# Gate and up of the dense layer by seven half-size products for eight, and the down projection by column halves

## The chip, the cores and the metric

The program runs on one core of one Trainium2 chip. The metric is the device time of one execution in microseconds (us); lower is better. All tensors are float32, and the profile lists every float32 matrix multiplication as two TensorE instructions, called records here: two weight loads (PEld) and two MATMULs (PE).

## The reference, cut to what matters

A model of two blocks. The second block has two layers; the first of them ends in a dense SwiGLU layer, and only that is touched. It works on 528 tokens (16 meta tokens and 512), width 1024, inner width 2816:

```
def swiglu(t, wg, wu, wd):
    return (jax.nn.silu(t @ wg) * (t @ wu)) @ wd

h = layer_norm(ALPHA * h + mix, ln1_g[i], ln1_b[i])
f = swiglu(h, ffn_w_gate[j], ffn_w_up[j], ffn_w_down[j])      # layer 0
h = layer_norm(ALPHA * h + f, ln2_g[i], ln2_b[i])
```

## The kernel before, in words

The program is a chain of stages. Each stage is a block with one instruction list for each engine, ordered by semaphores alone, and all engines meet at the block's end. The dense layer is `dense_ffn` (L2848), between `mix_layer` of layer 0 (L2713) and `project_and_attend` of layer 1 (L2351). It has two blocks.

**Up block.** The tokens stand as columns in `core.feat` (128 partitions, DK = 8 slices of the width, NTOK = 528 columns). The 2816 inner channels are FC = 22 chunks of 128. A chunk's weights, gate and up together, are 1 MB; `core.lead` holds two chunks, each in a buffer of its own, and `load_dense` (L2842) loads the first two during `mix_layer`. A hardware loop of 11 turns takes two chunks a turn. TensorE computes, for each chunk, gate and up (`a`) for both halves of the tokens (HALF = 264 columns): 4 banks of PSUM of 8 accumulated matmuls each, so 32 matmuls or 64 records a chunk (L2893). Two sets of four banks alternate. ScalarE applies SiLU to the gate (L2903), VectorE multiplies it by up and writes `hm` (L2911). SP loads the chunk after next when TensorE has left a buffer (L2873), and behind the last of them the down weights `wd`, in two column halves of 5.6 MB (L2877).

**Down block.** `norm` (`TokenNorm`, L2162) is the layer norm of a token tile. TensorE first multiplies the 16 meta tokens for both column halves of `wd` (L2930), then four token tiles of 128 with both halves in turn (L2938; 22 matmuls or 44 records of 512 columns into one bank). After each second half it transposes the tile normalised before (`norm.turn`, L2227). VectorE adds the residual (L2965), takes statistics (L2180) and normalises (L2186 to L2209); ScalarE takes roots and moves the transposes back to `core.feat` (L2219, L2235). SP loads the norm's gains (L2176) and the next stage's first weights into `core.lead` (L2348) at the block's start.

Elsewhere in this kernel `chunk_half` of `project_and_attend` (L2465) does the like of the up block, written out without a loop: 8 matmuls (16 records) of 264 columns, each time with one wait on a semaphore ahead and one increment behind, two banks in turn, ScalarE reading each (L2565), VectorE at work on a convolution (L2663).

Of the kernel before, what the change touches and what calls it, by code (L numbers as in the profile page):

```python
# [8 lines left out]
ACT = mybir.ActivationFunctionType  # L9
ALU = mybir.AluOpType  # L10
AX = mybir.AxisListType

P = 128
# [51 lines left out]
class Core:  # L65
# [2096 lines left out]
class TokenNorm:  # L2162
# [19 lines left out]
    def center(self, dve, n, mean_square=None):  # L2182
        t, r = self.rows[n]
        h, mv, rt = self.core.hid[0:r, t, :], self.mv[0:r, n, :], self.rt[0:r, n, :]
        dve.wait_ge(self.measured, 2 * n + 2)
# [26 lines left out]
    def normalize(self, dve, n, mean_square=None):  # L2212
        self.center(dve, n, mean_square)
        self.finish(dve, n)

    def root(self, act, n):
# [613 lines left out]
def quarter(g, rows=META):  # L2830
    return slice(g * (P // 4), g * (P // 4) + rows)
# [16 lines left out]
def dense_ffn(core, A, w_in, weights):  # L2848

    with ExitStack() as ctx:  # L2850
        sb = lambda name, *shape: core.sb(ctx, name, [P, *shape])
        w = core.lead[:, :, :].rearrange("p (b a) x -> p b a x", b=2)
        wd = sb("wd", 2, FC, BANK)
        hm = sb("hm", FC, NTOK)
        norm = TokenNorm(core, ctx, A, 2, [(TILES, META)] + ROWS[:TILES], core.feat)
        sg = norm.gb[:, :, 0:NTOK]
        wd_in = [core.sem("wd_in") for _ in range(2)]
        made, silu, taken, down, out, summed, small_made, small_out = (
            core.sem(x) for x in "made silu taken down out summed small_made small_out".split())

        def halves(ap):
            return ap.rearrange("p (a n) -> p a n", a=2)

        with ExitStack() as up:
            pp = core.ps(up, "pp", [P, 2, 2, 2, BANK])
            with core.block() as block:

                @block.sync
                def _(sp):
                    with sp.Fori(1, FC // 2) as r:  # L2870
                        for b in range(2):
                            sp.wait_ge(made, r * 2 + b + 1)
                            sp.dma_start(w[:, b, :, :].rearrange("p a x -> p (a x)"),  # L2873
                                         A["ffn_up_2"][bass.ds(r * 2 + b, 1)].rearrange("c p x -> p (c x)")).then_inc(w_in[b], 16)
                    wdv = A["ffn_down_2"].rearrange("(f p) n -> p f n", p=P)
                    for half in range(2):
                        sp.dma_start(wd[:, half, :, :], wdv[:, :, half * BANK:(half + 1) * BANK]).then_inc(wd_in[half], 16)  # L2877

                @block.gpsimd
                def _(pool):  # L2880
                    core.clear_retired(pool)

                @block.tensor
                def _(pe):
                    pe.sem_inc(made, 2)
                    with pe.Fori(0, FC // 2) as r:
                        for b in range(2):
                            pe.wait_ge(w_in[b], r * 16 + 16)
                            pe.wait_ge(taken, r * 2 + b + 1)
                            for a in range(2):  # L2890
                                for half in range(2):
                                    for k in range(DK):
                                        last = pe.matmul(pp[:, b, a, half, 0:HALF], w[:, b, a, k * P:(k + 1) * P],  # L2893
                                                         core.feat[:, k, half * HALF:(half + 1) * HALF], start=k == 0, stop=k == DK - 1)
                            last.then_inc(made, 1)

                @block.scalar
                def _(act):
                    with act.Fori(0, FC // 2) as r:
                        for b in range(2):  # L2900
                            act.wait_ge(made, r * 2 + b + 3)
                            act.wait_ge(taken, r * 2 + b + 1)
                            act.activation(halves(sg[:, b, :]), pp[:, b, 0, :, 0:HALF], ACT.Silu).then_inc(silu, 1)  # L2903

                @block.vector
                def _(dve):
                    dve.sem_inc(taken, 2)  # L2907
                    with dve.Fori(0, FC // 2) as r:
                        for b in range(2):
                            dve.wait_ge(silu, r * 2 + b + 1)  # L2910
                            dve.tensor_tensor(halves(hm[:, bass.ds(r * 2 + b, 1), :].rearrange("p a n -> p (a n)")),  # L2911
                                              halves(sg[:, b, :]), pp[:, b, 1, :, 0:HALF], ALU.mult).then_inc(taken, 1)

        po = core.ps(ctx, "po", [P, TILES, BANK])
        pm = core.ps(ctx, "pm", [P, 2, BANK])
        turned = core.ps(ctx, "turned", [P, 2, BANK])
        banks = [turned[:, a, :] for a in range(2)]
        with core.block() as block:

            @block.sync  # L2920
            def _(sp):
                norm.load(sp)
                weights.load(sp)

            @block.tensor
            def _(pe):
                for half in range(2):
                    pe.wait_ge(wd_in[half], 16)
                    for f in range(FC):
                        last = pe.matmul(pm[quarter(f % 4), half, :], hm[:, f, row_cols(TILES)], wd[:, half, f, :],  # L2930
                                         start=f < 4, stop=f >= FC - 4)
                    last.then_inc(small_made, 1)
                for n in range(2 * TILES):
                    t, half = divmod(n, 2)
                    if n >= TILES:
                        pe.wait_ge(out, n - TILES + 1)
                    for f in range(FC):
                        last = pe.matmul(po[:, n % TILES, :], hm[:, f, row_cols(t)], wd[:, half, f, :],  # L2938
                                         start=f == 0, stop=f == FC - 1)
                    last.then_inc(down, 1)  # L2940
                    if half:
                        norm.turn(pe, t, banks)
                norm.turn(pe, TILES, banks)

            @block.scalar
# [7 lines left out]
            @block.vector  # L2953
            def _(dve):
                for half in range(2):
                    dve.wait_ge(small_made, half + 1)
                    add_quarters(dve, core.hid[0:META, TILES, half * BANK:(half + 1) * BANK], pm[:, half, :], summed, half, small_out)
                    dve.wait_ge(small_out, half + 1)
                    norm.take_stats(dve, 0, half)
                norm.normalize(dve, 0)  # L2960
                for n in range(2 * TILES):
                    t, half = divmod(n, 2)
                    dve.wait_ge(down, n + 1)
                    h = core.hid[:, t, half * BANK:(half + 1) * BANK]
                    dve.scalar_tensor_tensor(out=h, in0=h, scalar=ALPHA, in1=po[:, n % TILES, :],  # L2965
                                             op0=ALU.mult, op1=ALU.add).then_inc(out, 1)
                    dve.wait_ge(out, n + 1)
                    norm.take_stats(dve, t + 1, half)
                    if half:
                        norm.normalize(dve, t + 1)  # L2970


UT = P // 2
# [635 lines left out]
```

## Time and profile before

| | us |
|---|---|
| runs | 3224.13, 3210.89, 3216.73 |
| median of the 3 runs | 3216.73 |
| span of the profiled execution, first to last instruction | 3206.7 |
| its own time | not given; the span is 10.0 below the median |
| up block's matmuls, L2893 | 1611.9 to about 1927.8 |
| down block, L2930 to the last transpose | 1929.7 to about 2102 |

A row of the profile names line, engine, operation, the tile written and the tiles read, then count, busy time and mean duration. Durations of matmuls overlap each other (a MATMUL of 386 ns starts every 0.22 us), so the pace is read from starts, not from durations. PEclk is the granted TensorE clock as a share of full speed (1.00 is 2.4 GHz, 0.50 is 1.2 GHz, between them a mix of the two).

### The profile page before, as it was taken

The page shows a single profiled execution, that of the slowest core. Times are in us where ns is not written, and L with a number is a line of the kernel's source. Part 1 is how long each engine was busy: PE and PEld are TensorE (multiplying, and loading weights), DVE is VectorE, ACT ScalarE, POOL GpSimd, SP SyncE. Part 2 cuts the span into 40 slices and gives each one's busy share as a digit, 9 for nine tenths or more (in the row PEclk, how much of TensorE's full clock was granted, in tenths as well). Part 3 has the DMA queues.
Part 4 walks back from the last instruction along what each step waited for, and adds up shares of the span by engine and source line. Part 5 has one row for each costly group of instructions (what it writes and reads, how often), then busy time and mean ns, then how long its engine had stood idle before and what let it go on. Part 6 is the DMA issues. An engine that isn't in the chain of part 4 may idle for free. (4 is left out here: it accounts for less than half of the span.)

```text
span 3206.7 us, 43786 instructions
## 1 busy us (share of the span) xinstructions
PE 2981.5 (93%) x18418; PEld 1840.9 (57%) x18418; DVE 1047.9 (33%) x1946; ACT 549.4 (17%) x1262; POOL 220.6 (7%) x204
## 2 busy tenths in 40 slices
PE   8998899998779979989999999999999799999897
PEld 5544788654343338867578884478776444444343
DVE  5666665653311233731400002109222311111014
ACT  3222333221111121133000000011240000000001
POOL 0001321340000000011000000000010100000000
PEclk9998899999879979999999999999999799999998
DMA  3411000116289931202012142011220614547917
GB/s 115 107 53 44 4 17 26 43 40 248 120 338 431 426 111 47 105 27 118 0 53 78 66 162 86 0 55 72 78 94 1 271 50 203 232 171 320 414 49 290
DMA packets 79478, 414.04 MB, mean 129 GB/s; under 512 B 10675, under 2 KB 16179, under 8 KB 63588
## 3 DMA queue, kind: packets, MB, share of 16 engines
q1 hardware_dynamic: 68028, 384.75, 30.3%
q10 hardware_dynamic: 7848, 14.61, 1.9%
q0 software_dynamic: 3456, 12.58, 1.0%
q8 instruction: 110, 1.80, 0.2%
q14 instruction: 36, 0.29, 0.0%
HBM read 383.17 MB, written 28.76 MB: 128 GB/s over the span
## 5 line engine op out<-in xcount | busy, mean ns | idle before, releaser
L3318 PE MATMUL pgu<-gu,xg 128*64 128x320 f32 (+1 forms) x2560 | 393.4, 462 | 8.9 <-POOLq L3246 8.9
L2893 PE MATMUL pp<-feat,lead 128*128 128x264 f32 x1408 | 315.8, 388 | 2.0 <-DVEq L2907 2.0
L3318 PEld LDWEIGHTS pgu<-gu,xg 128*64 128x64 f32 x2560 | 182.3, 137 | 204.7 <-issue 130.3
L2893 PEld LDWEIGHTS pp<-feat,lead 128*128 128x128 f32 x1408 | 269.0, 191 | 48.7 <-DVEq L2907 2.3
L312 PE MATMUL proj<-feat,w 128*128 128x512 f32 x576 | 254.4, 595 | 2.6 <-PEq L153 2.6
L2465 PE MATMUL ring<-feat,lead 128*128 128x264 f32 x1024 | 243.3, 397 | 3.0 <-PEq L2253 1.5
L2465 PEld LDWEIGHTS ring<-feat,lead 128*128 128x128 f32 x1024 | 198.1, 196 | 40.4 <-issue 6.2
L3325 PE MATMUL py<-down,hm_t 128*64 128x512 f32 x880 | 200.3, 603 | 10.0 <-POOLq L3246 10.0
L2465 PE MATMUL ring<-feat,w 128*128 128x264 f32 x896 | 209.4, 390 | 0.0
L2465 PEld LDWEIGHTS ring<-feat,w 128*128 128x128 f32 x896 | 169.1, 192 | 30.3 <-issue 2.4
L312 PEld LDWEIGHTS proj<-feat,w 128*128 128x128 f32 x576 | 106.7, 190 | 123.8 <-issue 123.8
L497 DVE SCALAR_TENSOR_TENSOR mixed<-padded,taps,mixed 128x512 f32<-128x512 f32 x216 | 162.4, 752 | 7.7
L2663 DVE SCALAR_TENSOR_TENSOR conv<-vg,cols,conv x240 | 163.3, 760 | 0.0
L2938 PE MATMUL po<-wd,hm 128*128 128x512 f32 x352 | 151.9, 593 | 0.0
L3325 PEld LDWEIGHTS py<-down,hm_t 128*64 128x64 f32 x880 | 62.0, 139 | 121.4 <-issue 104.6
L3387 DVE TENSOR_TENSOR hm<-sg,pgu 128x384 f32<-128x384 f32 (+1 forms) x40 | 20.8, 521 | 314.7 <-PE pgu L3318 209.1
L2911 DVE TENSOR_TENSOR hm<-gb,pp 128x528 f32 x22 | 15.5, 704 | 305.1 <-ACT gb L2903 305.1
L2938 PEld LDWEIGHTS po<-wd,hm 128*128 128x128 f32 x352 | 66.6, 190 | 83.2 <-issue 83.1
L2778 PE MATMUL pp<-wo,feat 128*128 128x512 f32 x256 | 111.3, 593 | 2.8 <-POOL feat L2827 2.8
L3270 ACT ACT_TABLE_LOAD x19 | 24.4, 1283 | 460.8 <-PE pgu L3318 280.3
L2778 PEld LDWEIGHTS pp<-wo,feat 128*128 128x128 f32 x256 | 48.1, 190 | 61.9 <-issue 61.9
L2219 ACT ACTIVATE rt<-rt 128x1 f32<-128x1 f32 (+1 forms) x15 | 3.0, 203 | 378.1 <-DVE rt L2189 378.1
(493 smaller groups left out, 3479.2 us busy)
## 6 DMA issues: line engine op xcount, KB each, us to landing
gu<-in_moe_gu SPq DMA_DIRECT2D x16, 3072.0 KB, 13.4
gu<-in_moe_gu SPq DMA_DIRECT2D x16, 2560.0 KB, 15.8
ring<-in_w_gate SPq DMA_DIRECT2D x16, 2048.0 KB, 13.6
ring<-in_w_up SPq DMA_DIRECT2D x16, 2048.0 KB, 15.5
ring<-in_w_down SPq DMA_DIRECT2D x16, 2048.0 KB, 17.7
w<-in_w_in SPq DMA_DIRECT2D x15, 2048.0 KB, 7.7
down<-in_moe_down SPq DMA_DIRECT2D x8, 3072.0 KB
lead<-in_ffn_up SPq DMA_DIRECT2D x22, 1024.0 KB, 4.8
```

What stands on the lines that cost most here:

```text
L312: last = pe.matmul(proj[:, n % 2, :], w[:, g % 2, k, c * P:(c + 1) * P], core.feat[:, k, :], start=k == 0, stop=k == DK - 1)
L497: dve.scalar_tensor_tensor(out=out, in0=src[:, j:j + SEQ], scalar=taps[:, n, j:j + 1], in1=out, op0=ALU.mult, op1=ALU.add).then_inc(convol ...
L2465: last = pe.matmul(ring[:, n % RINGS, 0:HALF], w[g % 2][:, c, k * P:(k + 1) * P], core.feat[:, k, cols(half)], start=k == 0, stop=k == DK - 1)
L2663: dve.scalar_tensor_tensor(out=out, in0=src[:, j:j + NTOK], scalar=tap(c, j), in1=out, op0=ALU.mult, op1=ALU.add).then_inc(own, 1)
L2778: last = pe.matmul(pp[:, n % 2, n // 2 % 2, 0, :], mixed[:, k, row_cols(t)], wo[:, k, half * BANK:(half + 1) * BANK], start=k == 0, stop=k ...
L2893: last = pe.matmul(pp[:, b, a, half, 0:HALF], w[:, b, a, k * P:(k + 1) * P], core.feat[:, k, half * HALF:(half + 1) * HALF], start=k == 0, ...
L2911: dve.tensor_tensor(halves(hm[:, bass.ds(r * 2 + b, 1), :].rearrange("p a n -> p (a n)")), halves(sg[:, b, :]), pp[:, b, 1, :, 0:HALF], AL ...
L2938: last = pe.matmul(po[:, n % TILES, :], hm[:, f, row_cols(t)], wd[:, half, f, :], start=f == 0, stop=f == FC - 1)
L3270: act.activation(sg[:, q, 0:n], pgu[:, 2 * q, 0:n], ACT.Silu).then_inc(silu, 1)
L3318: last = pe.matmul(pgu[half(h), part, 0:n], xg[:, k, :], w[:, k, h, :], start=k == 0, stop=k == DK - 1)
L3325: last = pe.matmul(py[half(h), :], hm_t[:, c, :], down[:, c, h * BANK:(h + 1) * BANK], start=c == 0, stop=c == XC - 1)
L3387: dve.tensor_tensor(hm[:, c0:c0 + n], sg[:, q, 0:n], pgu[:, 2 * q + 1, 0:n], ALU.mult).then_inc(multiplied, 1)
```

## The change

Two chunks of channels and two halves of the width and of the tokens make 2 x 2 x 2 blocks. In place of eight half-size products, seven are computed for gate and seven for up for each pair of chunks, on sums and differences of the weight blocks and of the token blocks (Strassen's method, in Winograd's form). Each product is 4 matmuls (8 records) of 264 columns. Three of the bank groups are read by ScalarE in the middle of the accumulation (a copy into SBUF), and more products are then added to the same bank; VectorE adds the copies to later contents.

For each pair: TensorE 14 products; ScalarE 6 copies and 4 SiLUs; VectorE 6 sums of a copy and a bank, 3 multiplications, and 4 sums of weight blocks (1024 elements a partition each). Once at the start VectorE forms 4 sums of token blocks (1056 elements each). The 11 pairs are written out, with no hardware loop. A second weight buffer `w_second` is added, and a pair is one load of 2 MB. The first half of the down weights (`wd0`) is loaded at the up block's start; the second (`wd1`) at the down block's start, ahead of the gains and the next stage's weights. The down block does all first column halves (meta, then four tiles), then all second halves. `core.feat`'s block x12 is overwritten by a difference; the temporaries lie in the norm's gain buffer.

The diff, cut to its core:

```diff
 def load_dense(core, A, sp, landed):
     for b in range(2):
...
-                     A["ffn_up_2"][b:b + 1].rearrange("c p x -> p (c x)")).then_inc(landed[b], 16)
+                     A["ffn_up_2"][b:b + 1].rearrange("c p x -> p (c x)")).then_inc(landed[0], 16)
...
                 def _(sp):
-                    with sp.Fori(1, FC // 2) as r:
-                        for b in range(2):
-                            sp.wait_ge(made, r * 2 + b + 1)
-                            sp.dma_start(w[:, b, :, :].rearrange("p a x -> p (a x)"),
...
-                    for half in range(2):
-                        sp.dma_start(wd[:, half, :, :], wdv[:, :, half * BANK:(half + 1) * BANK]).then_inc(wd_in[half], 16)
+                    load_pair(1)
+                    sp.dma_start(wd0[:, :, :], wdv[:, :, 0:BANK]).then_inc(wd_in[0], 16)
+                    for r in range(2, PAIRS2):
+                        sp.wait_ge(product, PRODUCTS * (r - 1))
+                        load_pair(r)
...
                 def _(pe):
-                    with pe.Fori(0, FC // 2) as r:
-                        for b in range(2):
-                            pe.wait_ge(w_in[b], r * 16 + 16)
-                            pe.wait_ge(taken, r * 2 + b + 1)
-                            for a in range(2):
-                                for half in range(2):
-                                    for k in range(DK):
...
+                    def multiply(bank, lhs, rhs, a, begin):
+                        for k in range(KH):
+                            last = pe.matmul(bank, lhs[:, a, k * P:(k + 1) * P], rhs[:, k, :], start=begin and k == 0,
+                                             stop=k == KH - 1, skip_group_check=True)
+                        last.then_inc(product, 1)
+
+                    for r in range(PAIRS2):
+                        pe.wait_ge(w_in[r % 2], 16 * (r // 2 + 1) + (16 if r % 2 == 0 else 0))
+                        if r >= 2:
+                            pe.wait_ge(opened, OPENED * (r - 2) + O21 + 1)
+                            pe.wait_ge(hidden, HIDDEN * (r - 2) + H21 + 1)
+                        for a in (GATE, UP):
+                            multiply(bank_x(r, a), weight(r, 0, 0), x11, a, True)
+                        if r:
+                            pe.wait_ge(added, SUMS * (r - 1) + S11_U + 1)
+                        for a in (GATE, UP):
+                            multiply(bank_y(a), weight(r, 0, 1), x21, a, True)
+                        pe.wait_ge(w_summed, 4 * r + 2)
+                        pe.wait_ge(x_summed, 2)
+                        for a, c in ((GATE, C1_G), (UP, C1_U)):
+                            pe.wait_ge(copied, COPIES * r + c + 1)
+                            multiply(bank_x(r, a), s2(r), t2, a, False)
+                        for a, c in ((GATE, S12_G), (UP, S12_U)):
+                            if r:
+                                pe.wait_ge(added, SUMS * (r - 1) + c + 1)
+                            multiply(bank_z(a), s1(r), t1, a, True)
+                        pe.wait_ge(w_summed, 4 * r + 4)
+                        pe.wait_ge(x_summed, 3)
+                        for a, c in ((GATE, C2_G), (UP, C2_U)):
+                            pe.wait_ge(copied, COPIES * r + c + 1)
+                            multiply(bank_x(r, a), s3(r), t3, a, False)
+                        for a, c in ((GATE, C5_G), (UP, C5_U)):
+                            pe.wait_ge(copied, COPIES * r + c + 1)
+                            multiply(bank_z(a), s4(r), x22, a, False)
+                        pe.wait_ge(x_summed, 4)
+                        for a, c in ((GATE, S22_G), (UP, S22_U)):
+                            pe.wait_ge(added, SUMS * r + c + 1)
+                            multiply(bank_x(r, a), weight(r, 1, 1), t4, a, False)
...
                 def _(act):
...
+                        copy(r, G_P1, c1[GATE], bank_x(r, GATE))
+                        copy(r, U_P1, c1[UP], bank_x(r, UP))
+                        act.wait_ge(added, SUMS * r + S11_G + 1)
+                        act.activation(c1[GATE], c1[GATE], ACT.Silu).then_inc(opened, 1)
+                        copy(r, G_P6, c2[GATE], bank_x(r, GATE))
+                        copy(r, U_P6, c2[UP], bank_x(r, UP))
+                        copy(r, G_P5, c5[GATE], bank_z(GATE))
+                        copy(r, U_P5, c5[UP], bank_z(UP))
...
                 def _(dve):
...
+                    sum_weights(0, (0, 1))
+                    sum_inputs()
+                    sum_weights(0, (2, 3))
+                    for r in range(PAIRS2):
+                        add(r, G_P2, C1_G, c1[GATE], bank_y(GATE))
+                        add(r, U_P2, C1_U, c1[UP], bank_y(UP))
+                        add(r, G_P7, C5_G, c5[GATE], bank_x(r, GATE))
+                        add(r, U_P7, C5_U, c5[UP], bank_x(r, UP))
+                        add(r, G_P3, C2_G, c2[GATE], bank_z(GATE))
+                        add(r, U_P3, C2_U, c2[UP], bank_z(UP))
+                        open_and(r, O22, S22_U)
+                        dve.tensor_tensor(hm[:, 2 * r + 1, HALF:], c5[GATE], c5[UP], ALU.mult).then_inc(hidden, 1)
+                        open_and(r, O12, S12_U)
+                        dve.tensor_tensor(hm[:, 2 * r, :], row1[GATE], row1[UP], ALU.mult).then_inc(hidden, 1)
+                        if r + 1 < PAIRS2:
+                            sum_weights(r + 1, (0, 1))
+                        dve.wait_ge(opened, OPENED * r + O21 + 1)
+                        dve.wait_ge(product, PRODUCTS * r + U_P4 + 1)
+                        dve.tensor_tensor(hm[:, 2 * r + 1, 0:HALF], open21, bank_x(r, UP), ALU.mult).then_inc(hidden, 1)
+                        if r + 1 < PAIRS2:
+                            sum_weights(r + 1, (2, 3))
...
             def _(sp):
+                sp.dma_start(wd1[:, :, :], wdv[:, :, BANK:]).then_inc(wd_in[1], 16)
                 norm.load(sp)
                 weights.load(sp)
...
-                for n in range(2 * TILES):
-                    t, half = divmod(n, 2)
-                    if n >= TILES:
-                        pe.wait_ge(out, n - TILES + 1)
...
+                    for t in range(TILES):
+                        if half:
+                            pe.wait_ge(out, t + 1)
+                        for f in range(FC):
+                            last = pe.matmul(po[:, t, :], hm[:, f, row_cols(t)], wd[half][:, f, :], start=f == 0, stop=f == FC - 1)
```

`bank_x(r, a)` is bank 2a + r % 2, `bank_y(a)` bank 4 + a, `bank_z(a)` bank 6 + a. `sum_weights(r, ...)` first waits for the pair's load and for the last product of the pair before that reads its targets (`U_P3`), then forms s1, s2, s4 and s3 in that order.

## Rows read from the trace of the kernel before

**Rows 1.** The page's part 1: busy us, share of the span, instructions.
```profile
PE 2981.5 (93%) x18418; PEld 1840.9 (57%) x18418; DVE 1047.9 (33%) x1946; ACT 549.4 (17%) x1262; POOL 220.6 (7%) x204
```
**Rows 2.** Windows, all engines: stretch, us, busy (x count) each, PEclk, DMA share, GB/s.
```profile
1612.00:1928.00 316.00, 315.76 (x1408) 268.95 (x1408) 14.79 (x21) 27.07 (x33) 0.00 (x0) 0.99 0.27 96
1928.00:1941.00 13.00, 10.45 (x88) 2.70 (x88) 4.11 (x6) 1.77 (x2) 0.00 (x0) 1.00 1.03 399
1941.00:2100.00 159.00, 155.34 (x390) 70.33 (x389) 28.99 (x46) 4.16 (x13) 0.00 (x0) 1.00 0.00 1
```
**Rows 3.** Timeline of ScalarE in the up block: start, us, line, operation, idle before.
```profile
1628.84 1.28 ACT L2903 ACT_TABLE_LOAD   x1 [17.80 <-PE pp L2893]
...
1913.62 1.28 ACT L2903 ACT_TABLE_LOAD   x1 [13.61 <-PE pp L2893]
...
1927.88 0.61 ACT L2903 ACTIVATE gb<-pp 128x528 f32<-128x528 f32 x1 [12.35 <-PE pp L2893]
```
**Rows 4.** Windows of L2893 alone: stretch, us, PE busy, PEld busy, PEclk, DMA.
```profile
1612.00:1640.50 28.50, 28.50 (x118) 24.00 (x119) 0.92 0.11 38
...
1657.30:1685.78 28.48, 28.48 (x130) 24.32 (x129) 1.00 0.21 74
```
**Rows 5.** Timeline of layer 0's projection: products of 16 records, written out, with VectorE busy.
```profile
1319.71 15.07 PE L2465 MATMUL ring<-feat,lead 128*128 128x264 f32 x67
1319.87 19.77 DVE L2663 SCALAR_TENSOR_TENSOR conv<-vg,cols,conv  x29
...
1320.58 0.39 ACT L2565 ACTIVATE gates<-ring 128x264 f32<-128x264 f32 x1 [3.17 <-PE ring L2465]
...
1341.94 0.39 ACT L2565 ACTIVATE gates<-ring 128x264 f32<-128x264 f32 x1 [3.17 <-PE ring L2465]
```
**Rows 6.** Windows of L2465 alone, the same stretch: columns as in rows 4.
```profile
1310.00:1345.00 35.00, 35.00 (x159) 29.90 (x158) 1.00 0.36 127
```
**Rows 7.** Groups by line and shape, whole span: VectorE and ScalarE operations of like size.
```profile
L1880 DVE TENSOR_TENSOR feat<-slot_t,hid 128x1024 f32<-128x1024 f32 x4 | 4.6, 1220 | 0.0
L2648 DVE TENSOR_TENSOR vg<-vg 128x528 f32<-128x528 f32 x8 | 5.7, 709 | 123.2 <-ACT vg L2565 123.2
L2671 DVE SCALAR_TENSOR_TENSOR conv<-ring,conv 128x264 f32<-128x264 f32 x16 | 5.8, 425 | 37.4 <-PE ring L2481 37.4
L1568 DVE TENSOR_TENSOR steps_and_weighted<-cst,scal 128x512 f32<-128x512 f32 x32 | 34.0, 1105 | 0.0
L2565 ACT ACTIVATE gates<-ring 128x264 f32<-128x264 f32 x64 | 24.8, 388 | 137.5 <-PE ring L2465 137.5
```
**Rows 8.** The page's part 6, loads: out<-in, queue, count, size, median us to landing.
```profile
w<-in_w_in SPq DMA_DIRECT2D x15, 2048.0 KB, 7.7
...
wd<-in_ffn_down SPq DMA_DIRECT2D x2, 5632.0 KB, 27.5
```
**Rows 9.** One line's own view, L2877 (the down weights' two loads): shortest, median, longest.
```profile
L2877 SPq DMA_DIRECT2D wd<-in_ffn_down x2: 390/5211/10032, 1900.0 to 1900.4; - x2
...
DMA to landing us min/median/max: 19.7/27.5/35.4
```
**Rows 10.** Timeline where the up block ends and the down block begins.
```profile
1928.63 0.70 DVE L2911 TENSOR_TENSOR hm<-gb,pp 128x528 f32 x1 [12.26 <-ACT gb L2903]
...
1929.72 5.33 PE L2930 MATMUL pm<-wd,hm 128*16 128x512 f32 x44 [1.96 <-PEq L2866]
...
1935.88 5.33 PE L2930 MATMUL pm<-wd,hm 128*16 128x512 f32 x44 [0.83 <-DMA wd<-in_ffn_down]
...
1941.14 38.03 PE L2938 MATMUL po<-wd,hm 128*128 128x512 f32 x88
```
**Rows 11.** Waits from 1600 to 2110: who for whom, us in total, times, longest.
```profile
DVE hid L2965 <- PE po L2938: 128.3, 8, 17.5
```
**Rows 12.** Windows, all engines, around the start of layer 1's projection: columns as in rows 2.
```profile
2100.00:2110.00 10.00, 8.52 (x28) 6.72 (x27) 0.00 (x0) 1.48 (x3) 0.20 (x1) 0.66 0.57 211
2110.00:2150.00 40.00, 40.00 (x181) 34.15 (x181) 1.42 (x2) 5.59 (x12) 0.00 (x0) 1.00 0.15 53
```

More of the change, by code:

```diff
@@ L2855, in dense_ffn @@
         norm = TokenNorm(core, ctx, A, 2, [(TILES, META)] + ROWS[:TILES], core.feat)
-        sg = norm.gb[:, :, 0:NTOK]
+        kept = norm.gb[:, :, :].rearrange("p a d -> p (a d)")
         wd_in = [core.sem("wd_in") for _ in range(2)]
[L2858 to L2862, printed above, removed]
-        with ExitStack() as up:
-            pp = core.ps(up, "pp", [P, 2, 2, 2, BANK])
+        down, out, summed, small_made, small_out = (core.sem(x) for x in "down out summed small_made small_out".split())
@@ L2897, in _, with copy @@
                 @block.scalar
                 def _(act):
[L2899 to L2903, printed above, removed]
+                    def copy(r, j, dst, bank):
+                        act.wait_ge(product, PRODUCTS * r + j + 1)
+                        act.activation(dst, bank, ACT.Copy).then_inc(copied, 1)
@@ L2905, in _, with sum_weights @@
                 @block.vector
                 def _(dve):
[L2907 to L2912, printed above, removed]
+                    def sum_weights(r, steps):
+                        for n in steps:
+                            if n == 0:
+                                dve.wait_ge(w_in[r % 2], 16 * (r // 2 + 1) + (16 if r % 2 == 0 else 0))
+                                if r:
+                                    dve.wait_ge(product, PRODUCTS * (r - 1) + U_P3 + 1)
+                                dve.tensor_tensor(s1(r), weight(r, 1, 0), weight(r, 1, 1), ALU.add).then_inc(w_summed, 1)
+                            else:
+                                dve.wait_ge(w_summed, 4 * r + n)
+                                out, x, y = {1: (s2(r), s1(r), weight(r, 0, 0)), 2: (s4(r), weight(r, 0, 1), s2(r)),
+                                             3: (s3(r), weight(r, 0, 0), weight(r, 1, 0))}[n]
+                                dve.tensor_tensor(out, x, y, ALU.subtract).then_inc(w_summed, 1)
@@ new lines, in sum_inputs, with add @@
+                    def sum_inputs():
+                        for n, (out, x, y) in enumerate(((t1, x12, x11), (t2, x22, t1), (t3, x22, x12), (t4, x21, t2))):
+                            if n:
+                                dve.wait_ge(x_summed, n)
+                            dve.tensor_tensor(out, x, y, ALU.subtract).then_inc(x_summed, 1)
+                    def add(r, j, c, dst, bank):
+                        dve.wait_ge(product, PRODUCTS * r + j + 1)
+                        dve.wait_ge(copied, COPIES * r + c + 1)
+                        dve.tensor_tensor(dst, dst, bank, ALU.add).then_inc(added, 1)
@@ L2914, in dense_ffn @@
+        wd1 = sb("wd1", FC, BANK)
+        wd = (wd0, wd1)
         po = core.ps(ctx, "po", [P, TILES, BANK])
@@ L2929, in _ @@
                     for f in range(FC):
[L2930 removed]
+                        last = pe.matmul(pm[quarter(f % 4), half, :], hm[:, f, row_cols(TILES)], wd[half][:, f, :],
                                          start=f < 4, stop=f >= FC - 4)
                     last.then_inc(small_made, 1)
[L2933 to L2942 removed]
+                    for t in range(TILES):
[3 more added lines that the diff above has]
+                            last = pe.matmul(po[:, t, :], hm[:, f, row_cols(t)], wd[half][:, f, :], start=f == 0, stop=f == FC - 1)
+                        last.then_inc(down, 1)
+                        if half:
+                            norm.turn(pe, t, banks)
                 norm.turn(pe, TILES, banks)
@@ L2959, in _ @@
                     norm.take_stats(dve, 0, half)
[L2960 to L2968, printed above, removed]
-                    if half:
-                        norm.normalize(dve, t + 1)
+                    if half:
+                        norm.normalize(dve, 0, taken=len(norm.rows) + 1)
+                    for t in range(TILES):
+                        n = half * TILES + t
+                        dve.wait_ge(down, n + 1)
+                        h = core.hid[:, t, half * BANK:(half + 1) * BANK]
+                        dve.scalar_tensor_tensor(out=h, in0=h, scalar=ALPHA, in1=po[:, t, :],
+                                                 op0=ALU.mult, op1=ALU.add).then_inc(out, 1)
+                        dve.wait_ge(out, n + 1)
+                        norm.take_stats(dve, t + 1, half)
+                        if half:
+                            norm.normalize(dve, t + 1, taken=len(norm.rows) + t + 2)
 UT = P // 2
```

82 lines of the change are left out of this document (70 added, 12 removed).

## Prediction

> **What bounds the kernel now.** I read the page's busy shares first: TensorE is busy 93% of the span, VectorE 33%, ScalarE 17% [rows 1]. A mean says nothing of one stage, so the windows come next. In the up block TensorE is busy 315.76 of 316 us, VectorE 14.8, ScalarE 27.1, DMA 0.27 of its time; the down block is the same picture [rows 2]. So a record taken from TensorE is time taken from the end, as long as the rest, which grows a lot, stays hidden.
>
> Then the pace. The table loads of SiLU come once a loop turn; eleven of them lie between 1628.84 and 1913.62, so a turn is 284.78 / 10 = 28.48 us [rows 3]. It holds 128 records (two chunks of 64): 0.2225 us a record, at a clock of 1.00 [rows 4]. The first 28.5 us hold 118 records where a later turn's window counts 130, at 0.92 [rows 4]: a start at the lower level that costs 12 x 0.2225 = 2.7 us, before and after alike.
>
> **What is removed.** The new pair has 14 products of 4 matmuls, 14 x 8 = 112 records for 128; 11 pairs have 1232 for 1408. The shape stays 128x264, so 176 x 0.2225 = 39.2 us go.
>
> **Many small groups.** The new code waits and increments about every 8 records (154 times; before, 22 times). No row has groups of 8 records of this shape. Nearest is the projection: written out, a wait and an increment every 16 records, two banks read by ScalarE in turn, VectorE at work on SBUF beside it. ScalarE's reads are (1341.94 - 1320.58) / 6 = 3.56 us apart, again 0.2225 a record, at 1.00 [rows 5, 6]. So waits long satisfied cost nothing I can see at 16, and neither does loop against written-out code. Lower bound 0: the loop shows no overhead to win back. Upper bound: one handover a product. From ScalarE's SiLU (ends 1928.49) to VectorE's start at 1928.63 that is 0.14 us [rows 3, 10]; 154 x 0.14 = 21.6 us. I take 0, since the projection is by far the likest row.
>
> The Trainium skill, TensorE: Matmul & The Clock Gate, section The cost: per-tile semaphore tail, says that increments of matmuls finish one after another, 26.3 ns each. By that, 132 more increments would cost an estimated 3.5 us and the gain would be 3.5 us smaller; the trace does not bear it out for matmuls that follow one another, since one increment in 16 records and one in 64 run at the same pace [rows 3, 5].
>
> **What is added beside TensorE.** The pair takes 112 x 0.2225 = 24.9 us, a product 1.78. I count from the pair's start; product n ends at 1.78n, in the order P1, P2, P6, P5, P7, P3, P4, each gate then up.
>
> ScalarE: 6 copies and 4 SiLUs of 264 elements at 0.39 [rows 7], 3.9 us of 24.9. VectorE: 6 sums and 2 multiplications of 264 at 0.43, one of 528 at 0.71, 4 weight sums of 1024 at 1.22 [rows 7]: 3.4 + 0.7 + 4.9 = 9.0 us. Neither is near 24.9, so only the order can hurt:
> - P6 gate (starts 7.1) adds to the bank of P1 gate. The copy is done by 1.8 + 0.4 + two handovers = 2.5. Slack 4.6.
> - P7 gate (14.2) needs the copy of P6 gate (ends 8.9): about 9.6. Slack 4.6. P3 gate (17.8) needs the copy of P5 gate (12.5): 13.2.
> - P4 gate (21.4) needs VectorE's sum of P7 gate (16.0): 16.7. Slack 4.7.
> - The next pair's P6 (at 24.9 + 7.1 = 32.0) needs s1 and s2, which VectorE may begin once P3 up has ended (21.4). In front of them stand a sum, a multiplication of 264 and one of 528; with the two sums 0.43 + 0.43 + 0.71 + 2.44 = 4.0 of 10.6 us. s3 and s4 follow P4 up: 24.9 + 0.43 + 2.44 = 27.8, wanted at 39.1.
> - First pair: s1, s2 and four token sums (1056 elements; I take 1.25) and s4, s3 are 9.9 us before VectorE takes its first add. P6 wants the first four by 7.1 (4.9), P7 all by 14.2. Behind them ScalarE's SiLU and the copy of P6 gate come at 9.9 + 0.43 + 0.39 + 0.39 = 11.1, some 11.6 with handovers. Slack 2.6, the tightest place, and the low clock there adds to it. Here lies the far bound of a VectorE sum: the slowest SBUF sum in the trace is 1.105 us for 512 elements [rows 7], so 2.2 for 1024. Eight of them end at 17.7, and P7 would be some 5 us late, once; in later pairs 6.0 of 10.6 still fits.
>
> So everything added is priced at nothing, covered by TensorE's 24.9 us a pair; if the cover went, its price would be each lateness itself, pair by pair.
>
> **Loads.** A pair is 2 MB. Such loads land in 7.7 us [rows 8], and pair r+1's buffer is asked for at the start of pair r and wanted at 21.4: slack 13.7. At the block's start SP issues pair 1 and then wd0, 5.6 MB; one of the two down loads, issued together, landed in 19.7 us, though SP was held 10.0 us in issuing one of them [rows 9]. The queue is free before pair 2 is asked for at 24.9. In the down block wd1 is issued at its start, ahead of the gains and the next stage's weights; it has the meta rows, 5.3 us, and four tiles at 38.03 / 2 = 19.0 each [rows 10], 81 us, and wants about 20. The gains behind it are needed after that too. The next stage wants its weights some 165 us on.
>
> **The seams.** Before, the last product was followed by SiLU (1927.88) and a multiplication ending 1929.33 [rows 3, 10], 1.5 us after the last product. Now the gate's SiLU runs beside P4 up, and one multiplication of 264 remains: 0.43 plus a handover. 1.0 us goes. TensorE's wait of 0.83 us for the second down half goes as well [rows 10]. A second change from meta rows to full tiles is added; the row shows 1935.88 + 5.33 to 1941.14, no gap, so 0 [rows 10]. In the down block VectorE waited 128.3 us for TensorE [rows 11], TensorE never for VectorE; with the halves apart, a bank is read four tiles before it is reused, and the last tile's normalisation has the same length. 0. The start of the up block has fewer registers to set and a longer code; TensorE's idle at the like seam is 1.96 us [rows 10], so between 2 us won and 2 lost; I take 0.
>
> **Sum.** 39.2 + 1.0 + 0.8 = 41.0 us. The profiled span, 3206.7, becomes 3165.7. That execution's own time is not given; its span lies 10.0 below the median of the runs, 3216.73, and I carry that over: 3175.7 us. About 0.5% (16 us) is what a measurement of this kernel tells from no change.
>
> **Rivals.**
> 1. *Each group pays a handover.* TensorE does not run ahead over the waits, and each product begins 0.14 us late: 21.6 us back, 3197.3. For it: no row has groups as short. Against: the projection [rows 5, 6]. Chance 0.10.
> 2. *The chain through VectorE and ScalarE becomes the bound* (slower than before). Place: each pair's s1 and s2 for the next P6, or in the first pair the sums before P7. It decides once TensorE loses over 41.0 / 11 = 3.7 us a pair, so when the 4.0 us of VectorE's work in that place take 14.3, 3.6 times my rows. At four times, 16.0 us, 5.4 are lost a pair, 59 in all: 3235. Against: the worst row gives 6.0. Chance 0.03.
> 3. *The clock falls.* At the lower level a record takes twice as long, so 184 of the 1232 records at that level eat the whole gain. The level was mixed, 0.66, where TensorE started after a break, and 1.00 in the next stretch [rows 12]; if each pair had idling enough to run 30 of its records so, 11 x 30 x 0.2225 = 73 us are lost, 3249. Against: rows 5 and 6 change banks each 3.56 us at 1.00. Chance 0.03. The Trainium skill, TensorE: Matmul & The Clock Gate, section A second HAM failure mode: psum-queue depth-cycling, has this rule: going round PSUM's banks with small idle times between groups makes the clock swing and takes throughput. By that rule this rival would be the outcome; rows 5 and 6 disagree so far.
> 4. *A load comes late, or the gain is lost elsewhere.* 2 MB would have to take 21.4 us for a first stall; within 0.5%: 3217. Chance 0.02.
> 5. *The change does not do what it says:* counted in the code, 14 calls of 4 matmuls a pair leave 112 records; chance under 0.01, in rival 4.
>
> The forecast keeps 0.82.
>
> **How the numbers follow.** Forecast 3175.7. Low end: the start's 2.0, and the 5.8 by which the lowest run lies below the median: 3168. High end: the handover's whole bound, 3197. Forecast and rival 1 make 0.92 faster, and of the rest a mild form of 2 or 3 leaves some gain: faster 0.93, same 0.03, slower 0.04.
>
> **What would show it.** L2893's successor with 1232 records, and the first SiLU's of two pairs 24.9 us apart; a clock of 1.00 from the second pair on; TensorE's idle inside the block near 0, with at most a piece in the first pair; the block's matmuls ending near 1888.6; no wait for `wd`. A spacing of 26.9 would be rival 1; idle time on TensorE put down to `sums_w` or `kept` rival 2; PEclk under 0.95 rival 3; idle put down to a DMA rival 4.

## The result and the profile after

The changed kernel takes 3177.33 us (median of 4 runs, 3173.29 to 3178.81), the kernel before 3214.92 beside it (4 runs). The ratio is 0.9879, 95% interval 0.9864 to 0.9893. Forecast was 3175.7, in a range of 3168 to 3197. The profiled execution took 3173.29 us around a span of 3171.5.

The windows of the changed kernel's dense layer, all engines (columns as in [rows 2]): the up block, the first meta rows, the rest of the down block.

```profile
1618.00:1895.00 277.00, 276.83 (x1232) 235.77 (x1232) 99.11 (x146) 45.35 (x111) 0.00 (x0) 0.99 0.26 97
1895.00:1901.00 6.00, 5.08 (x45) 1.43 (x44) 0.43 (x1) 1.28 (x1) 0.00 (x0) 1.00 0.65 208
1901.00:2068.00 167.00, 162.43 (x438) 72.64 (x436) 32.41 (x51) 5.04 (x15) 0.00 (x0) 0.99 0.12 46
```

Against [rows 2]: 1408 records in 316 us have become 1232 in 277. TensorE is as full as it was. VectorE has gone from 14.8 us to 99.1 in that stretch and ScalarE from 27.1 to 45.4, and neither is seen in TensorE's time. That is the whole change in one row.

The timeline around the first change of pairs, weight loads left out (start, us, engine, line, operation, idle before):

```profile
1618.17 1.23 DVE L3019 TENSOR_TENSOR sums_w<-lead 128x1024 f32<-128x1024 f32 x1 [2.66 <-PEq L2741]
1618.17 9.90 PE L2947 MATMUL pp<-feat,lead 128*128 128x264 f32 x32 [1.49 <-PEq L2741]
...
1624.96 1.28 ACT L2996 ACT_TABLE_LOAD   x1
...
1626.87 1.22 DVE L3024 TENSOR_TENSOR lead<-lead 128x1024 f32<-128x1024 f32 x1
...
1629.89 0.39 ACT L2988 ACTIVATE gb<-pp 128x264 f32<-128x264 f32 x1 [1.00 <-PE pp L2947]
...
1635.03 3.72 PE L2947 MATMUL pp<-feat,lead 128*128 128x264 f32 x16
...
1643.66 1.22 DVE L3019 TENSOR_TENSOR sums_w<-w_second 128x1024 f32<-128x1024 f32 x1
...
1644.92 1.22 DVE L3024 TENSOR_TENSOR sums_w<-sums_w,w_second 128x1024 f32<-128x1024 f32 x1
1645.71 7.28 PE L2947 MATMUL pp<-feat,w_second 128*128 128x264 f32 x32
...
1647.76 0.39 ACT L2988 ACTIVATE gb<-pp 128x264 f32<-128x264 f32 x1 [3.23 <-PE pp L2947]
...
1652.83 7.28 PE L2947 MATMUL pp<-sums_x,sums_w 128*128 128x264 f32 x32
...
1654.81 0.39 ACT L2988 ACTIVATE gb<-pp 128x264 f32<-128x264 f32 x1 [2.67 <-PE pp L2947]
...
1659.95 3.72 PE L2947 MATMUL pp<-feat,w_second 128*128 128x264 f32 x16
...
1872.03 0.39 ACT L2988 ACTIVATE gb<-pp 128x264 f32<-128x264 f32 x1 [3.23 <-PE pp L2947]
```

Read it as a set of deadlines. The second pair's P1 begins at 1645.71; VectorE ends s2 at 1644.92 + 1.22 = 1646.14, 0.43 us after that, and P6, which needs it, begins at 1652.83: 6.7 us to spare. The room is smaller for the copy of P6 gate: it ends at 1654.81 + 0.39 = 1655.20, and P7, which needs it, begins at 1659.95, 4.75 us later. In the first pair the eight sums end at 1628.09, 9.9 us after the block's start, and P6 gate's copy ends at 1630.28, 4.75 us before P7 at 1635.03. The copies of P1 gate in pairs two and eleven, 1647.76 and 1872.03, are nine pairs apart: 24.92 us a pair, 0.2225 a record. The one idle time in the list of TensorE is that of the block's start. The granted clock is 0.88 from 1618 to 1640, where the first 32 records take 9.90 us and later ones 7.28, and 1.00 from 1640 to 1895.

The seams, where the up block ends and where the layer ends:

```profile
1895.18 0.43 DVE L3059 TENSOR_TENSOR hm<-gb,pp 128x264 f32<-128x264 f32 x1 [2.24 <-PE pp L2947]
...
1896.00 5.33 PE L3082 MATMUL pm<-wd,hm 128*16 128x512 f32 x44 [0.92 <-PEq L2925]
...
1901.26 49.19 PE L3089 MATMUL po<-wd,hm 128*128 128x512 f32 x114
...
2065.12 1.97 PE L2227 MATMUL turned<-cst,hid 128*128 128x128 f32 x8 [3.65 <-DVE hid L2209]
...
2068.57 6.65 PE L2465 MATMUL ring<-feat,lead 128*128 128x264 f32 x17 [1.48 <-PEq L3069]
```

TensorE's idle at the seam is 0.92 where it was 1.96 [rows 10], and the wait for `wd` is gone.

Stage by stage, from these starts (before: 1611.9, 1929.7, 2102.1, span 3206.7):

| stretch | before | after | difference |
|---|---|---|---|
| start to the up block's first matmul | 1611.9 | 1618.2 | +6.2 |
| up block to down block | 317.8 | 277.8 | -40.0 |
| down block to layer 1's projection | 172.4 | 172.6 | +0.2 |
| from there to the end | 1104.6 | 1102.9 | -1.7 |
| span | 3206.7 | 3171.5 | -35.2 |

The layer itself gives 39.8 us. The 6.2 us ahead of it, in code that is the same in both, want an explanation, and so does the 0.2 in the down block. The last row needs none: over thirteen profiles of all kernels here that stretch takes between 1102.7 and 1106.7 us, in either kernel.

### The profile page after: what moved, and what is told of

It is laid out like the page before. It is cut to its first block and busy times, and to the rows that moved or that the text cites. A ratio compares the mean times of both kernels' runs of the same rounds, so it can differ in the third digit from the quotient of the medians.

```text
span 3171.5 us, 43527 instructions
## 1 busy us (share of the span) xinstructions
PE 2946.1 (93%) x18242; PEld 1809.0 (57%) x18242; DVE 1131.1 (36%) x2071; ACT 567.5 (18%) x1340; POOL 221.1 (7%) x204
## 5 line engine op out<-in xcount | busy, mean ns | idle before, releaser
L2465 PE MATMUL ring<-feat,lead 128*128 128x264 f32 x1024 | 242.6, 397 | 3.0 <-PEq L3069 1.5
L2465 PEld LDWEIGHTS ring<-feat,lead 128*128 128x128 f32 x1024 | 197.6, 196 | 40.4 <-issue 6.3
L2465 PE MATMUL ring<-feat,w 128*128 128x264 f32 x896 | 209.4, 390 | 0.0
L2465 PEld LDWEIGHTS ring<-feat,w 128*128 128x128 f32 x896 | 169.1, 192 | 30.3 <-issue 2.4
L3035 DVE TENSOR_TENSOR gb<-gb,pp 128x264 f32<-128x264 f32 x66 | 28.2, 429 | 174.8 <-PE pp L2947 174.8
L2947 PE MATMUL pp<-sums_x,sums_w 128*128 128x264 f32 x352 | 80.1, 386 | 0.0
L2947 PEld LDWEIGHTS pp<-sums_x,sums_w 128*128 128x128 f32 x352 | 66.9, 190 | 11.4
```

What stands on the lines that cost most here:

```text
L2465: last = pe.matmul(ring[:, n % RINGS, 0:HALF], w[g % 2][:, c, k * P:(k + 1) * P], core.feat[:, k, cols(half)], start=k == 0, stop=k == DK - 1)
L2947: last = pe.matmul(bank, lhs[:, a, k * P:(k + 1) * P], rhs[:, k, :], start=begin and k == 0, stop=k == KH - 1, skip_group_check=True)
L3035: dve.tensor_tensor(dst, dst, bank, ALU.add).then_inc(added, 1)
```

## The experiments

My theory: TensorE's count of records is the time, and all that was added is covered with slack that can be counted. The rivals: the gain comes in part from elsewhere (the loop's removal, the order of the down block); or the cover is thin (groups, sums, reads or loads near their limit); or stops bring the clock down.

**The kernel before once more (e1_before_again).** No edit.

> The kernel before, unchanged, for a second profile. The changed kernel's profile reached the dense layer 6.2 us later than the first profile of before did, in code that is the same in both. If that is scatter of the earlier stages, this profile begins the up block's matmuls somewhere from 1611 to 1619 us; if the new program costs time ahead of the layer (longer code, other loads), it begins within 1 us of 1611.9. Up block start to down block start 317.8 us, down block start to the projection of layer 1 172.4 us, both within 0.5 us: these hold no scatter by either theory.

Measured: one run of 3218.81 us, span 3217.1. The view of L2893 alone:

```profile
L2893 PE MATMUL pp<-feat,lead x1408: 385/386/803, 1621.8 to 1937.4; 128*128 128x264 f32 x176
```

The unchanged kernel reaches the layer at 1621.8, 9.9 us later than in its first profile and 2.8 beyond the range that I had given scatter. Over thirteen profiles of all kernels here that start lies between 1611.9 and 1624.9, for forms of the kernel before between 1611.9 and 1621.8, for forms of the changed one between 1612.9 and 1624.9. So the 6.2 us lie within the scatter of the stages before, and the first profile of before reached the layer earliest of all. A cost of the new program of a microsecond or two ahead of the layer could not be told from that scatter. The up block again takes 317.9 us. The down block took 173.4, a microsecond over what I expected, for the reason at the end of this section.

**The down block's order alone (e2_down_order_alone)**, in the kernel before:

```diff
-                for n in range(2 * TILES):
-                    t, half = divmod(n, 2)
+                    for t in range(TILES):
```

> The kernel before with only the down block's order changed (all first column halves, then all second; loads as before). My theory: only TensorE's wait of 0.83 us for the second half of wd goes, so down block start to layer 1's projection falls from 172.4 us to 171.6, and the time stays within 0.1% of before. A rival, that the order itself is worth some of the gain (less waiting on normalisation), would show 5 us or more below before.

Measured: 3213.58 us, ratio 1.0005 (0.9995 to 1.0015). The wait for `wd` is gone, yet the down block takes 172.6 us (1930.8 to 2103.4) and not the 171.6 expected; 0.88 of that microsecond is the last transposes, told of below. The order by itself is worth nothing that the runs could show.

**The old order in the changed kernel (e3_old_down_order)**: the same lines turned back, `wd1` still loaded at the block's start.

> The changed kernel with the old order of the down block (tile by tile, both halves), the second half of wd still loaded at the down block's start. My theory: TensorE needs wd1 5.3 us after the block's start and it lands after about 15 to 20 us (19.7 us with another load of its size beside it before), so TensorE stands idle 10 to 14 us once, and after that break the clock is low for some us more: 12 to 17 us slower than the changed kernel, 3190 us. The rival, that the order does not matter since loads are fast enough, expects under 3 us.

Measured: 3186.61 us, ratio 0.9928 (0.9911 to 0.9944), about 0.5% or 16 us above the changed kernel's ratio. The timeline of that down block:

```profile
1890.71 5.33 PE L3082 MATMUL pm<-wd,hm 128*16 128x512 f32 x44 [0.92 <-PEq L2925]
...
1908.69 6.75 PE L3082 MATMUL pm<-wd,hm 128*16 128x512 f32 x44 [12.65 <-DMA wd<-in_ffn_down]
```

TensorE stands 12.65 us, and the 44 records behind the stop take 6.75 us where they took 5.33. The down block is 185.6 us, 13 to 14 more than in the changed kernel. So the new order has a job: not to save time, but to let `wd1` be loaded so late. In the code the second weight buffer and the sums are given back at the up block's end, and `wd1` is laid out only then.

**The loop written out, nothing else (e4_before_written_out):**

```diff
-                    with pe.Fori(0, FC // 2) as r:
+                    for r in range(FC // 2):
```

and so on SP, ScalarE and VectorE.

> The kernel before with the up block's hardware loop written out on all four engines, nothing else. My theory: the loop costs nothing, 128 records in 28.48 us with or without it; up block start to down block start 317.8 us give or take 0.5, time as before within 0.2%. The rival, that part of the 40 us gained in the up block is the loop's branches and the table load it repeats, expects 5 us or more less.

Measured: 3215.03 us, ratio 1.0008 (0.9999 to 1.0018); the up block 317.7 us. One table load is left of eleven, and the up block is no shorter for it. None of the gain is the loop's.

**Four more sums a pair (e5_four_more_sums)** in the place where P6 waits for VectorE:

```diff
+                                for n in range(4 if r else 0):
+                                    dve.tensor_tensor(s1(r), weight(r, 1, 0), weight(r, 1, 1), ALU.add).then_inc(again, 1)
+                                    dve.wait_ge(again, 4 * (r - 1) + n + 1)
```

> The changed kernel with VectorE forming s1 five times instead of once in each pair after the first: 4 more sums of 1024 elements, 1.26 us each, in the place where the next pair's P6 waits. My theory, from the changed kernel's profile: s2 ends 0.43 us after the pair's first record and P6 begins at 7.12; with 4 x 1.26 = 5.0 more it ends at 5.5, still in time, so nothing changes: 112 records in 24.92 us, time as the changed kernel's, ratio to before 0.988. The rival, that VectorE's added work already costs TensorE something (reads of SBUF beside it, or waits close to their limit), expects the pair to lengthen by 0.3 us or more, 3 us in all.

Measured: 3171.84 us, ratio 0.9869 (0.9853 to 0.9886), the up block 277.9 us. Doubling VectorE's sums of weights costs nothing.

**Eight more (e6_eight_more_sums):** the same with 8.

> The same with 8 more sums, 10.1 us: s2 ends at 10.5, P6 wanted it at 7.12. My theory of the chain: TensorE stands idle 3.4 to 3.6 us in each of 10 pairs, 35 us in all, and no other wait appears (VectorE's sum of P2 comes at 13.9, the copy of P6 gate at 14.7, P7 gate at 17.8). With the rival of the clock on top, each such stop lets the granted clock fall to the lower level for some us after it, and a pair loses 5 to 7 us, 50 to 70 in all, with PEclk under 0.9. If neither, the idle time is under 2 us a pair.

Measured: 3220.1 us, ratio 1.0021 (1.0009 to 1.0032): the whole gain is gone, and a little more. The up block takes 325.1 us (1617.41 to 1942.5), 47.3 more. TensorE's timeline at three of the ten P6:

```profile
1655.52 9.07 PE L2948 MATMUL pp<-sums_x,sums_w 128*128 128x264 f32 x32 [3.28 <-DVE sums_w L3028]
1685.67 7.39 PE L2948 MATMUL pp<-sums_x,sums_w 128*128 128x264 f32 x32 [3.28 <-DVE sums_w L3028]
1714.13 9.08 PE L2948 MATMUL pp<-sums_x,sums_w 128*128 128x264 f32 x32 [3.28 <-DVE sums_w L3028]
```

And windows of TensorE behind the first two of these stops (stretch, us, busy, PEclk, DMA share, GB/s):

```profile
1655.50:1675.00 19.50, 19.48 (x80) 0.91 0.00 1
...
1685.60:1703.50 17.90, 17.83 (x80) 1.00 0.00 1
```

The chain part came as forecast: P6 begins 10.57 us after the pair's first record (1644.95), 3.45 late, ten times, 34.5. Most of the rest is the clock: behind a stop of 3.28 us the next 32 records took 9.07 us in seven pairs of ten (0.91 over the first of these windows) and 7.39 in three (1.00 over the second). That is 1.7 us each, 12 in all. The last microsecond is 0.10 us of restart in each pair (7.39 for 7.28). So both theories held part of it, and the full 50 to 70 of the clock rival did not come. This is my slower rival made real, in the place I gave it. By the prediction's count of that place 4.0 + 8 x 1.26 us stand in 10.6, so 3.5 us a pair would be lost; 3.45 were, and the clock's share came on top.

**Six more (e9_six_more_sums):** the same with 6.

> The changed kernel with 6 more sums of s1 a pair, between the 4 that cost nothing and the 8 that cost 47 us in the up block (34.5 of waiting, 12 of low clock after stops of 3.3 us). My theory, a chain with a fixed end: with 8 more, s2 ended 10.51 us after the pair's first record and P6 began 0.06 us later; two sums of 1.255 us less put P6 at 8.06 where TensorE reaches it at 7.12, so 0.94 us a pair and 9.4 us in all; stops as short as this leave the clock at 1.00, so up block start to down block start is 287.2 us against 277.8. The rival, that any stop in each pair brings the clock down, expects some 12 us more than that, 299 us.

Measured: 3183.13 us, ratio 0.9899 (0.9881 to 0.9917), up block 288.0 us (1620.49 to 1908.5) for 287.2 expected.

```profile
1647.91 7.28 PE L2948 MATMUL pp<-feat,w_second 128*128 128x264 f32 x32
1655.95 7.39 PE L2948 MATMUL pp<-sums_x,sums_w 128*128 128x264 f32 x32 [0.76 <-DVE sums_w L3028]
1663.17 3.72 PE L2948 MATMUL pp<-feat,w_second 128*128 128x264 f32 x16
```

P6 begins at 8.04, as worked out (8.06), and the records behind the stop run at full pace but for 0.10 us of restart (1663.17 - 1655.95 = 7.22 for 7.12). A stop of 0.76 us did not touch the clock (1.00 from 1650 to 1908). Between four extra sums that are free and six that are not lies the counted slack of 6.7 us in this place, 5.3 sums.

**A wait and an increment at every matmul (e7_every_matmul):**

```diff
+                            if k:
+                                pe.wait_ge(w_in[0], 32)
...
+                            if k < KH - 1:
+                                last.then_inc(ticks, 1)
```

> The changed kernel with a wait on a semaphore long satisfied ahead of every matmul of a product but the first, and an increment behind every matmul: 3 x 154 = 462 more waits and 462 more increments. My theory, that satisfied waits and increments cost nothing while TensorE runs ahead: 112 records in 24.92 us, no change. A handover's price of 0.14 us would give 65 us more. The Trainium skill, TensorE: Matmul & The Clock Gate, section The cost: per-tile semaphore tail, has 26.3 ns for each increment that queues; by it alone 462 would be an estimated 12.2 us more, 1.1 us a pair.

Measured: 3170.86 us, ratio 0.9863 (0.9847 to 0.9880), the up block 277.8 us (1616.68 to 1894.5). 462 more waits and increments cost nothing. That settles the widest unknown of the prediction. The 26.3 ns an increment that the Trainium skill gives for small matmuls packed as tiles into one array (TensorE: Matmul & The Clock Gate, The cost: per-tile semaphore tail) do not show here, in a stream of full-size matmuls that start every 0.445 us.

**The reads exposed (e8_read_exposed):** P6 right behind P1, gate then up.

```diff
-    (G_P1, U_P1, G_P2, U_P2, G_P6, U_P6, G_P5, U_P5, G_P7, U_P7, G_P3, U_P3, G_P4, U_P4) = range(14)
+    (G_P1, G_P6, U_P1, U_P6, G_P2, U_P2, G_P5, U_P5, G_P7, U_P7, G_P3, U_P3, G_P4, U_P4) = range(14)
```

and the calls of `multiply` in that order.

> The changed kernel with the products in the order P1 gate, P6 gate, P1 up, P6 up, and so on: nothing stands between a product and the next one into the same bank, so ScalarE's read of the bank is exposed twice a pair. My theory: from the first record of P1 to the end of the copy is 2.44 us in the changed kernel's profile, and 0.14 us of handover follow, where P6 would begin at 1.78: 0.8 us each time, 22 times 17.6 us; in the first pair P6 waits for the sums as well (s1, s2 and two token sums, 5.0 us), some 2 us more: 18 to 21 us in all, a pair of 26.5 us. The rival, that the order of the products hides nothing (TensorE would not have waited anyway), expects under 3 us; a clock that falls from such small stops, 25 us or more a pair, 3400 us.

Measured: 3196.32 us, ratio 0.9945 (0.9929 to 0.9962); the up block 296.2 us (1624.94 to 1921.1), 18.4 more, within the 18 to 21 expected.

```profile
1656.05 0.39 ACT L2987 ACTIVATE gb<-pp 128x264 f32<-128x264 f32 x1 [3.23 <-PE pp L2947]
1656.59 2.02 PE L2947 MATMUL pp<-sums_x,sums_w 128*128 128x264 f32 x8 [0.64 <-ACT gb L2987]
1658.44 1.94 PE L2947 MATMUL pp<-feat,w_second 128*128 128x264 f32 x8
```

Only the order of the list differs, and nearly half of the gain goes. The idle time now names ScalarE's copy as what ended it. The clock stayed up behind stops of 0.57 to 0.64 us here too (1.00 from 1655 to 1921).

**The loads asked for 14.2 us later (e10_load_later):**

```diff
-                        sp.wait_ge(product, PRODUCTS * (r - 1))
+                        sp.wait_ge(product, PRODUCTS * (r - 1) + U_P5 + 1)
```

> The changed kernel with each pair's load (from the third pair on) asked for only when the pair before has done 8 of its 14 products, 14.2 us later than in the changed kernel. My theory: the load lands in 7.7 to 7.9 us, so 22.1 us after the pair's start, and VectorE first reads it at 22.9 (in the changed kernel's profile, 2.05 us before the next pair): no change, up block start to down block start 277.8 us, but only 0.8 us is left of 15. The rival, that the loads are near the bound already and a second buffer is what the change lives on, expects waits of VectorE and TensorE on the load and 5 us or more.

Measured: 3174.97 us, ratio 0.9871 (0.9852 to 0.9891), the up block 277.7 us.

```profile
1661.74 0.37 SPq L2930 DMA_DIRECT2D lead<-in_ffn_up  x1
...
1670.17 1.22 DVE L3019 TENSOR_TENSOR sums_w<-lead 128x1024 f32<-128x1024 f32 x1
```

The load is issued at 1661.74 and VectorE reads it at 1670.17, 8.4 us later, at the moment at which it would have read it anyway. Loads are not near the bound: with the 14.2 us taken from them they still come in time.

**The changed kernel once more (e11_after_again).** No edit.

> The changed kernel unchanged, for its ratio beside before on one chip and a second profile. Up block start to down block start 277.8 us, down block start to layer 1's projection 171.7 or 172.6 us (the last transposes at either level of the clock), ratio 0.987 to 0.988. The up block begins anywhere from 1611 to 1622 us, as in the profiles so far of either kernel.

Measured: 3176.63 us (5 runs), ratio 0.9883 (0.9867 to 0.9900); up block begins at 1618.88 and takes 277.4 us, the down block 171.7. The ratio lies just above the 0.987 to 0.988 expected.

The down block's microsecond is explained by the last transposes. They wait 3.65 us or 3.66 us for the last tile's normalisation, and then take either 1.09 us (three profiles of thirteen: the first of before, e3, e11) or 1.97 (the other ten, among them the second of before and the first of the changed kernel, where the granted clock from 2065 to 2068 is 0.50):

```profile
2073.79 1.09 PE L2227 MATMUL turned<-cst,hid 128*128 128x128 f32 x8 [3.66 <-DVE hid L2209]
...
2109.66 1.97 PE L2227 MATMUL turned<-cst,hid 128*128 128x128 f32 x8 [3.66 <-DVE hid L2209]
```

The first row is of e3, the second of the kernel before, unchanged, in e1. Both kernels show both, so the 0.88 us belong to the execution and not to the change. Like with like, the two blocks take 490.2 us before and 449.1 in e11 (transposes of 1.09 in both), 491.3 in e1 and 450.4 in the first profile after (1.97 in both): the layer gives 41.1 or 40.9 us.

## Why the prediction was right, and where it was off

- *176 records at 0.2225 us, 39.2.* Right: 1232 records, 24.92 us a pair, and TensorE without a stop after its first record. The rate read from the turns of the loop [rows 3] and from the projection [rows 5] held to the last digit.
- *Small groups at 0, bound 21.6.* Right, and e7 closes it at three further waits and increments a group. Rival 1 falls, with the spacing of 24.92 and with e7.
- *VectorE and ScalarE covered.* Right, and by the deadlines as worked out: s2 was put at about 0.5 us into the next pair and came at 0.43, the first pair's sums at 9.9 us and came at 9.9. One thing was overlooked: SiLU's table load of 1.28 us falls into the first pair between the copies and the first SiLU. It is hidden, since ScalarE had to wait there for VectorE's sum. The first pair's slack of 2.6, called the tightest place, came out at 4.75 us, no less than in the second pair: its first 32 records ran 2.6 us longer at the lower clock, and P7 began so much later. Rival 2 was judged rightly in its first place, s1 and s2 for the next P6: it has the room that was worked out, and e6 overfills it. The tighter places (4.7 us, for the copy of P6 gate and, 1662.36 to 1667.07, the sum of P7 gate) were not filled by any run.
- *Loads.* Right: 7.6 to 8.9 us to landing, and e10 takes 14.2 us of the slack away without a cost.
- *Seams, 1.0 + 0.8.* 40.0 us between the starts of the two blocks against 39.2 + 1.0. The 0.8 is in the trace as a wait that is gone, but in the sum of this profile 0.88 us of the last transposes at the lower clock level hide it.
- *The start of the up block, 0.* TensorE's idle there is 1.49 where it was 2.02: 0.5 us that I had left at nothing.
- *Sum 41.0.* The layer gave 39.8 in the two first profiles, and 40.9 or 41.1 where the last transposes ran alike. Of the runs, 3214.92 - 3177.33 = 37.6, whose interval by the ratio, 34 to 44, holds 41.0; e11 gave 36.8. The whole times are too scattered to confirm the sum to a microsecond; the starts of the blocks do.
- *10.0 us from span to median.* The number was right to carry and wrong as a reading. What lies around a span is 1.7 to 3.0 us in every run (3173.29 for 3171.5; 3218.81 for 3217.1). The first profile of before was of an unusually quick execution: of the 41 runs of that kernel beside the experiments one has a shorter span. So the 10.0 was scatter between executions and no part of the kernel, and that is why the difference of the two spans, 35.2, understates the layer's 39.8.
- *The clock, rival 3.* It did not fall. By the Trainium skill's section A second HAM failure mode: psum-queue depth-cycling (TensorE: Matmul & The Clock Gate) small idle times between groups bring it down. Here groups into changing banks leave no idle time at all, and where e8 and e9 make stops of 0.57 to 0.76 us in every pair it stays up; e6's 3.28 us bring it down in seven pairs of ten. So in this kernel changing banks alone did not bring it down, with or without short stops. Why it held in the other three pairs of e6 no run shows.

No version among the experiments beats the changed kernel clear of the scatter: those that equal it (e5, e7, e10) add or delay work that was already hidden. The same method for the projections (1920 records of L2465) was not tried; VectorE has the convolution to do there.

## What to carry to other kernels

When one engine is full and the others are not, count its instructions and multiply by the pace between starts; then give each added step a deadline in that engine's time, and look for the smallest slack. An exchange of 176 records for 44 sums of weights, 4 of tokens, 66 copies and 66 adds is good as long as each has such a deadline, and what keeps them there is the order of the list: with three other products (5.3 us) between a product and the next one into its bank, a read of 0.4 us costs nothing, with none it costs 0.8. A change of order that saves nothing by itself (the down block's) can be what pays for the SBUF of the change that does.

## What was not expected of the hardware

Waits already satisfied and increments behind every float32 matmul (two records of 0.2225 us) left the pace the same to 0.1 us in 277. Behind a stop of TensorE of 3.28 us the next records ran at either level, from one pair to the next (9.07 us or 7.39 for 32 records), and behind one of 3.66 us from one execution to another (1.97 us or 1.09 for 8 transposes); behind stops of 0.57 to 0.76 us they ran at 1.00 each time. The stages ahead of the layer scatter by up to 13 us between executions of the same instructions, a third of the gain measured here, so a difference of two spans has to be taken stage by stage.
